# A gated feed-forward stage: fifteen column tiles of seven products in runs of four, in place of fourteen in runs of three

## The reference, cut to what matters

```python
def _conv_ffn(h, prev, w_gate, w_up, conv_w, conv_b, w_down):
    t = h.shape[1]
    gate_in = h @ w_gate
    buf = jnp.concatenate([prev.astype(gate_in.dtype), gate_in], axis=1)
    conv = conv_b
    for j in range(CONV_W):
        conv = conv + conv_w[j] * buf[:, j:j + t]
    out = (jax.nn.gelu(conv) * (h @ w_up)) @ w_down
    return out, buf[:, -(CONV_W - 1):]
```

## Time and profile before

| | |
|---|---|
| median of 3 runs | 853.72 us (852.87 to 855.38) |
| the profiled execution's own time | 855.38 us |
| its span, first to last instruction | 853.6 us |
| TensorE busy (matmul records) | 819.5 us, 96% |
| VectorE busy | 532.1 us, 62% |
| ScalarE busy | 382.4 us, 45% |
| GpSimd busy | 200.8 us, 24% |

### The profile page before, as it was taken

The page is one execution under the profiler, slowest core; times in us unless marked ns, Lnnn a source line. Parts: engine busy times, 40 slices in busy tenths (PEclk is TensorE's granted clock), DMA queues, the critical chain, the costliest instruction groups (busy, mean ns, idle before and its releaser), DMA issues.

```text
span 853.6 us, 17206 instructions
## 1 busy us (share of the span) xinstructions
PE 819.5 (96%) x7342; PEld 774.0 (91%) x7342; DVE 532.1 (62%) x828; ACT 382.4 (45%) x589; POOL 200.8 (24%) x157
## 2 busy tenths in 40 slices
PE   5999999998999999998999999999999999999996
PEld 5989999887989999984589999999999999999995
DVE  6969998898357635122325988888888868310013
ACT  6534414667655325122324755555555458322221
POOL 4100001110550251430025130202020224845430
PEclk9999999999999999999999999999999999999998
DMA  8211212625655394219402322323222233333302
GB/s 335 75 52 50 76 50 100 204 83 168 186 175 156 114 413 149 93 48 376 167 26 99 99 75 100 99 100 99 99 100 100 99 124 100 124 99 99 105 1 101
DMA packets 31294, 104.99 MB, mean 123 GB/s; under 512 B 3930, under 2 KB 7002, under 8 KB 28786
## 3 DMA queue, kind: packets, MB, share of 16 engines
q1 hardware_dynamic: 31218, 103.90, 35.8%
HBM read 96.28 MB, written 6.71 MB: 121 GB/s over the span
## 4 chain that ended last, share of the span: by engine, by line
PE 77%; DVE 12%; ACT 4%; DMA 4%; issue 2%; SPq 1%; POOL 0%; DVEq 0%; ACTq 0%
PE pj L696 15%; PE pj L698 15%; PE pj L697 15%; PE aux L703 3%; PE aux L705 3%; DMA w_raw<-in 3%; PE aux L704 3%; PE pj L703 3%; PE pj L705 3%; PE pj L704 3%; PE aux L1245 2%; PE pj L1314 2%; DVE h_lo L1913 1%; PE pj L1022 1%; DVE a_lo L2522 1%
## 5 line engine op out<-in xcount | busy, mean ns | idle before, releaser
L660 POOL TENSOR_TENSOR w_lo<-w_raw,w_hi 128x512 fp32r<-128x512 f32 x106 | 146.1, 1401 | 492.7 <-ACT w_hi L1458 492.6
L696 PE MATMUL pj<-h_hi,w_hi 128*128 128x260 f32 x720 | 206.8, 287 | 11.0 <-POOL w_lo L660 9.6
L698 PE MATMUL pj<-h_hi,w_lo 128*128 128x260 f32 x720 | 203.9, 283 | 0.0
L697 PE MATMUL pj<-h_lo,w_hi 128*128 128x260 f32 x672 | 190.0, 283 | 0.0
L1458 ACT ACTIVATE w_hi<-w_raw 128x1024 fp32r<-128x1024 f32 x78 | 82.5, 1057 | 180.9 <-PE pj L698 147.9
L696 PEld LDWEIGHTS pj<-h_hi,w_hi 128*128 128x128 f32 x720 | 136.0, 189 | 13.3 <-POOL w_lo L660 9.6
L698 PEld LDWEIGHTS pj<-h_hi,w_lo 128*128 128x128 f32 x720 | 136.1, 189 | 0.0
L697 PEld LDWEIGHTS pj<-h_lo,w_hi 128*128 128x128 f32 x672 | 127.0, 189 | 0.3
L660 POOL TENSOR_TENSOR wx_lo<-w_raw,wx_hi 128x512 fp32r<-128x512 f32 x36 | 48.2, 1368 | 102.7 <-ACT wx_hi L1458 102.7
L2589 DVE TENSOR_TENSOR conv<-pj,rinv 128x520 f32<-128x520 f32 x7 | 4.9, 700 | 79.7 <-PE pj L698 79.7
L696 PE MATMUL pj<-h_hi,wx_hi 128*128 128x260 f32 x176 | 49.9, 283 | 0.8 <-DVE h_lo L1913 0.8
(11 more groups left out here) (484 smaller groups left out, 2345.3 us busy)
## 6 DMA issues: line engine op xcount, KB each, us to landing
w_raw<-in SPq DMA_DIRECT2D x126, 512.0 KB, 3.6
caches<-in SPq DMA_DIRECT2D x14, 1024.0 KB, 11.9
vpg<-in SPq DMA_DIRECT2D x16, 256.0 KB, 3.0
kpg<-in SPq DMA_DIRECT2D x12, 256.0 KB, 2.9
x<-in SPq DMA_DIRECT2D x4, 520.0 KB, 7.2
out<-x SPq DMA_DIRECT2D x16, 130.0 KB, 1.9
out<-kT SPq DMA_DIRECT2D x1, 1040.0 KB
far<-in SPq DMA_DIRECT2D x1, 1024.0 KB, 4.7
```

The source lines that it names most:

```text
L660: nc.gpsimd.tensor_tensor(lo[:, part], w_raw[:, raw_of(n) % 4, part], hi[:, part].bitcast(F32), ALU.subtract).then_inc(lo_done, 1)
L696: pe.matmul(out, s_hi, m_hi_, start=first, stop=False)
L697: pe.matmul(out, s_hi, m_lo_, start=False, stop=False)
L698: ins = pe.matmul(out, s_lo, m_hi_, start=False, stop=last)
```

## The change

One expression and two constants change: a run now has up to four tiles and begins every five tiles, and the numbers of the units after the gated stage move by two, since there is one seven-product tile more (four units in place of two).

```diff
-    0, 4, 8, 12, 16, 26, 34, 42, 50, 58, 130, 154)
+    0, 4, 8, 12, 16, 26, 34, 42, 50, 58, 132, 156)
 R_GU, R_DOWN, R_END = 58, 102, 126
 
-RUNS = tuple((c, tuple(range(c + 1, min(c + 4, FT - 1)))) for c in range(2, FT - 2, 4))
+RUNS = tuple((c, tuple(range(c + 1, min(c + 5, FT - 1)))) for c in range(2, FT - 2, 5))
```

## The result

The changed kernel takes **859.07 us** (median of 13 runs), the kernel before 854.42 us beside it: the ratio is 1.0052, with a 95% interval of 1.0040 to 1.0064. It is slower by 3.4 to 5.5 us; forecast were +4.3 us and 858.0 us, the latter on a median of 853.72 us that is 854.42 us with more runs.

The account below looks back on a forecast made before the run. TensorE bounds the kernel, so time changes only with its matmuls or waits. Matmuls -1.44, added waits +5.28, queues 0 and tail +0.47 us sum to +4.3 us on 853.72: 858.0 us, range 855.0 to 861.0.

Parts of the forecast that it names:

- Matmuls, -1.44 us: TensorE: one plain tile fewer means 12 matmuls fewer at 0.12 us from start to start, -1.44 us.
- The run of three's 0.79 us: Third tile of a run: TensorE loses 0.79 us before third and fifth products, four times before and after, net 0.
- The second middle tile, 1.76 us a run: Runs of four: VectorE's lag grows again, TensorE loses 1.76 us more than in a run of three, +5.28 us over three.
- the third product's: Fourth tile of a run: TensorE waits for ScalarE's copy before the third product and loses 1.05 us.
- The tail, +0.47 us: Tile 20: the gate's scaling on VectorE takes 1.64 us beside GpSimd instead of 1.17, delaying the down projection 0.47 us.
- ScalarE's in-order queue hands VectorE's lag to TensorE: Third tile of a run: ScalarE's copies queue behind operations waiting for VectorE, so TensorE loses 0.35 and 0.44 us.
- VectorE's list is the period: Middle tiles of a run: VectorE takes 11.84 us per tile against TensorE's 10.08, so the lag grows by 1.76 us.
- rival (a): Gated stage: VectorE does its middle list within TensorE's 10.08 us, lag absorbed, 852.3 to 852.8 us; chance 0.09.
- (b): Fourth tiles: the lag repeats but doesn't grow, 0.79 us paid again, +1.4 us, 855.1 us; chance 0.07.
- (d): Gated stage: the run-long waits vanish by a shift of order and the matmuls go too, 849.1 us; chance 0.02.
- (c): Each run: later VectorE falls under one more of GpSimd's subtractions, 1.26 us, giving 861.8 us; chance 0.04.
- The 6 us of cover given to the weight loads: SP's loads for tile 10 would land about 575, ScalarE wants them at 581.25: 6 us of cover, cost 0.

Follow-up runs that it names:

- the kernel that changes nothing else: Kernel before with its runs of tiles in the order 2, 3, 3, 3, 3, same tiles and matmuls: 855.59 us, ratio 1.0019.
- the early copies: ScalarE's copies after first and third products moved ahead in third and fourth tiles: 851.17 us on the kernel before, 854.25 us on the changed kernel.
- the one long run: Changed kernel with RUNS set to one run of 18 seven-product tiles (3 to 20): 872.52 us, ratio 1.0211 to the kernel before.
- the last three kernels: Changed kernel with all copies early and read_mid before sum_corners, 852.98 us; that with a low part sooner, 852.12 us; changed kernel with low parts on GpSimd, 863.06 us.
- the completed order: Changed kernel with ScalarE's copies early, bank 2's right behind the Gelu, and read_mid ahead of sum_corners and behind one low part less: 852.98 us, ratio 0.9979.
- the next kernel: All copies early, read_mid before sum_corners, plus VectorE's last low part ahead of read_first in a run of four's last tile: 852.12 us, ratio 0.9972.

## Why the prediction was right

Forecast +4.3 us; measured +3.4 to +5.5 us by the runs (medians +4.65), +3.99 us in the stage. The 0.7 us between medians and stage are within the interval and not explained; the forecast lies between the two. By its steps:

- **Matmuls, -1.44 us.** Twelve fewer on the page, steps of 0.12 us as before. By the record's 0.28 us the change would have saved 3.4 us, and the stage would be +2.0 us; +3.99 us shows the step to be the price.
- **The run of three's 0.79 us, four times before and after: right.** After: 0.35 and 0.45 us in tile 20 too.
- **The second middle tile, 1.76 us a run: 1.64 measured** (0.27 + 0.92 + 0.46, 1.65 in the second run). The seventh product's 0.27 us is exact, the fifth's 0.44 became 0.46. The mis-sized term is the third product's, 1.05 against 0.92: the spacing from sum_corners to read_mid was taken as 1.24 us from tile 8, and is 1.14 us in tile 10. The trace of the kernel before tells why. The last matmul of tile 8's fifth product there:

```profile
573.23 0.28 PE L705 MATMUL pj<-f_hi,w_lo 128*128 128x260 f32 x1
```

It ends at 573.51, and read_mid starts at 573.55: in tile 8 VectorE had just caught up with TensorE and started read_mid on its release, 0.10 us later than by its own list.
- **The tail, +0.47 us: +0.50 in the changed kernel** (the loss goes from 0.69 to 1.19 us), +0.44 in the kernel that changes nothing else. The scaling of tile 20's gate in the changed kernel took the forecast's 1.64 us:

```profile
704.95 1.64 DVE L2517 TENSOR_TENSOR gate<-gate,rinv 128x520 f32<-128x520 f32 x1
```
- **Sum of the measured terms:** -1.44 + 3 x 1.64 + 0.50 = +3.98, the stage's +3.99.
- **Reasons.** That ScalarE's in-order queue hands VectorE's lag to TensorE was right, shown by the early copies (-3.17 us on the kernel before). That VectorE's list is the period was half of it: the list is 10.5 us, the loop through ScalarE makes 11.72. The answer to rival (a), that 11.2 us would remain without the waits, took VectorE's waits from tile 8 (0.21 and 0.41 us), where it was less late; in a late tile they are 0.72 and 0.40 us, and 10.5 us remain, which is still over 10.08.
- **Rivals.** (a), (b) and (d) are excluded by the one long run and by the breaks in the trace. (c) did not occur in the changed kernel, the scaling took 1.64 to 1.67 us at the end of each run, as after the runs of three before; longer VectorE operations beside GpSimd appear once the order is altered (the last three kernels).
- The 6 us of cover given to the weight loads held in the changed kernel. In the completed order the loads for the next run's first tile came late (VectorE waited 1.52 us), a cover that the forecast had not priced; the next kernel shows that they cost little, for with 1.18 us less waiting there the stage gained 0.12 us, and its trace puts the rest on GpSimd's contention.

## What to carry to other kernels

Price a change by the step from one start to the next on the engine that bounds, and then carry the helpers' spacings over one more turn of the pattern: a helper that is late once, and in step again thanks to a lighter tile, falls back by its whole surplus when the heavier tile comes a second time (1.64 us here, where the first cost 0.79). Where the bounding engine waits for a small copy, look at what stands ahead of it in its in-order queue: moving the copies was worth 3.2 us, more than the 1.44 us of twelve matmuls. Work taken off a helper gains nothing if it stands just ahead of one of its own waits, which then grows by as much, and an idle engine that contends with the helper can cost more than it takes over.

## What the runs showed of the hardware that was not expected

GpSimd's operations lengthen even a very small one of VectorE's: 1.25 us for 8 columns of two SBUF inputs, where 0.16 us is usual. And two operations of 256 columns on GpSimd cost 3.2 us over seven tiles, through one VectorE operation issued 0.08 us too late. SBUF — State Buffer, Who interferes with whom, of the Trainium skill says that the port pair which the two engines share is an exclusive lock, that a VectorE operation with two SBUF inputs contends with a GpSimd one that reads SBUF, and that the order of issue decides who is blocked. The trace agrees. GpSimd needs 1.26 us for 512 columns, so by my estimate some 0.63 us for 256: its first operation holds from 594.15 to 594.78, VectorE's tap, issued at 594.23, ends at 595.43, 0.65 us later, and GpSimd's second ends 0.60 us after that, at 596.03.
